# Attention output by channel for pairs of heads, with the probabilities divided before they are turned

## The reference

```python
sc = (q_nope @ k_nope.T + q_rope @ k_rope.T) * scale     # masked by chunks of 64 frames
p = softmax(sc)                                          # p = exp(sc - max) / sum
y_b[:, h] = p @ v[:, h]                                  # queries x 64 channels
y_b = y_b * rsqrt(mean over the 64 channels of y_b ** 2 + eps) * out_norm[G:2 * G]
x = x + concat(y_a, y_b, y_c, y_d) @ w_out
```

## Time and profile before

| | us |
|---|---|
| median of 3 runs | 911.15 (910.9 to 911.25) |
| the profiled execution | 911.08 |
| its span, first to last instruction | 909.3 |
| TensorE busy | 894.7 |
| VectorE, ScalarE, GpSimd busy | 522.9, 220.2, 512.3 |

### The profile page before, as it was taken

One profiled execution on the slowest core, in us unless ns is written; L12 is line 12 of the kernel. 1 busy time (PEld: TensorE's weight loads), 2 busy tenths in 40 slices (PEclk: granted clock), 3 DMA queues, 4 the chain that ended last, 5 costly groups with the idle time before them and its releaser, 6 DMA issues.

```text
span 909.3 us, 15558 instructions
## 1 busy us (share of the span) xinstructions
PE 894.7 (98%) x5980; PEld 815.3 (90%) x5980; DVE 522.9 (58%) x1032; ACT 220.2 (24%) x485; POOL 512.3 (56%) x514
## 2 busy tenths in 40 slices
PE   8999999999999999999999999999999999999998
PEld 6997878678999999999979878866799999999998
DVE  6677858725656565522366776685465656563221
ACT  3334345432000000100133433464300000000001
POOL 6852483315866666666457244902287666666770
PEclk9999999999999999999999999999999999999999
DMA  9969321248554544333444873130855555443421
GB/s 276 275 106 122 90 77 65 52 90 229 139 139 137 140 137 135 128 128 129 129 133 140 31 152 94 48 95 6 185 139 139 140 139 139 140 128 128 142 90 35
DMA packets 159091, 112.92 MB, mean 124 GB/s; under 512 B 9829, under 2 KB 156682, under 8 KB 158890
## 3 DMA queue, kind: packets, MB, share of 16 engines
q1 hardware_dynamic: 154402, 104.44, 40.0%
q0 software_dynamic: 3984, 6.74, 7.2%
q10 hardware_dynamic: 632, 0.75, 0.3%
HBM read 108.33 MB, written 2.27 MB: 122 GB/s over the span
## 4 chain that ended last, share of the span: by engine, by line
PE 86%; DVE 9%; ACT 2%; issue 1%; DMA 1%; SPq 0%; DVEq 0%; ACTq 0%
PE ps L1313 53%; PE ps L899 7%; PE ps L865 6%; PE ps L1272 6%; PE ps L1331 2%; PE ps L885 2%; PE ps L1085 2%; PE ps L1054 1%; PE ps L1117 1%; PE ps L1210 1%; DMA arena<-in_x_sample 1%; PE ps L1218 1%; DVE work L2240 1%; DVE work L2079 1%; DVE arena L2183 0%
## 5 line engine op out<-in xcount | busy, mean ns | idle before, releaser
L674 POOL TENSOR_TENSOR work<-ring 128x512 f32<-128x512 f32 (+1 forms) x66 | 81.8, 1239 | 157.6 <-issue 113.4
L1313 PE MATMUL ps<-mixT,ring 128*128 128x160 f32 x672 | 105.0, 299 | 0.0
L1313 PE MATMUL ps<-hT,work 128*128 128x160 f32 x672 | 98.5, 299 | 0.0
L1313 PE MATMUL ps<-hT,ring 128*128 128x160 f32 x672 | 98.1, 299 | 0.0
L1313 PEld LDWEIGHTS ps<-mixT,ring 128*128 128x128 f32 x672 | 95.8, 190 | 0.0
L1313 PEld LDWEIGHTS ps<-hT,ring 128*128 128x128 f32 x672 | 93.7, 190 | 0.3
L1313 PEld LDWEIGHTS ps<-hT,work 128*128 128x128 f32 x672 | 93.7, 190 | 0.0
L675 POOL TENSOR_TENSOR ring<-ring 128x512 f32<-128x512 f32 (+1 forms) x66 | 82.4, 1248 | 5.2
L677 POOL TENSOR_TENSOR work<-ring,work 128x512 f32<-128x512 f32 (+1 forms) x66 | 82.1, 1244 | 5.2
L676 POOL TENSOR_TENSOR work<-ring 128x512 f32<-128x512 f32 (+1 forms) x66 | 82.0, 1242 | 5.2
L1764 ACT ACTIVATE arena<-ps 128x160 f32<-128x160 f32 x42 | 12.8, 304 | 286.9 <-PE ps L1313 286.9
(11 more groups left out here) (447 smaller groups left out, 1631.5 us busy)
## 6 DMA issues: line engine op xcount, KB each, us to landing
ring<-in_w_gu SPq DMA_DIRECT2D x88, 512.0 KB, 5.2
ring<-in_w_in SPq DMA_DIRECT2D x44, 512.0 KB, 6.4
ring<-in_w_down SPq DMA_DIRECT2D x32, 512.0 KB, 4.5
ring<-in_w_out SPq DMA_DIRECT2D x16, 512.0 KB, 4.9
ring<-in_w_down SPq DMA_DIRECT2D x16, 384.0 KB, 3.8
cst<-in_consts POOLq DMA_DIRECT2D x1, 1664.0 KB, 11.7
ring<-in_w_in SPq DMA_DIRECT2D x2, 640.0 KB, 5.5
arena<-r POOLq DMA_DIRECT2D x8, 160.0 KB, 18.0
```

The lines of the kernel that those rows point to most:

```text
L674: step(tt(s3, a11, a21, ALU.subtract))
L1313: ins = mm(bank(use, at * HT, HT), left, right(k), start=(opens and k == 0 and at == 0), stop=(closes and k == n - 1), skip_group_check=True)
```

## The change

Group B's output is made by channel for two heads at a time, as group C's is. ScalarE gets `shares(h)` behind `exponentials(h)`: it inverts the row sums (Ln, then Exp of the negative) and multiplies the probabilities by them in three parts; the turning waits for that. `weigh_values(p)` runs for heads 0 and 1 in `between(2)` and for heads 2 and 3 after the last head; for that there are two buffers of turned probabilities. ScalarE's `head_squares(p)`, TensorE's `head_mean(p)` and ScalarE's `head_rstd(p)` give 1/rms, and VectorE's `head_result(p)` writes `mixT` tile 2 + p. `b_out`, `group_tail`, `group_tail2`, the turning `bT` and `group_out` for group B go. Product 7 of `rg` moves ahead of the last turning. ScalarE's `exponentials(1)` moves ahead of `conv_input(0)`. On TensorE `pair_mean(1)` and `project(4)` move ahead of the wait for `h_sq`, and on ScalarE `pair_rstd(1)` moves ahead of that square. `pair_out` uses the shared helper `column_pair`; its products stay as they are.

```diff
@@ -155,8 +155,10 @@
...
         u += [(n, (0 if n == "rvt0" else 1,)) for n in fill[h]]
+        if h == 2:
+            u += [("bo0", (7,))]
         if h == H - 1:
-            u += [("rga", (0,)), ("rgb", (1,))]
+            u += [("rga", (0,)), ("rgb", (1,)), ("bm0", (6,))]
...
@@ -164,11 +166,12 @@
...
             u += [("ga0", (6,)), ("gx0_", (2,)), ("ga1", (3,)), ("gx1_", (7,)), ("rgc", (6,))]
-        u += [(f"bo{h}", (7,))]
-    u += [("rkt", (4, 5)), ("bT", (6, 7))]
+        if h == H - 1:
+            u += [("bo1", (7,))]
+    u += [("rkt", (4, 5)), ("bm1", (6,))]
...
     d("lg0", "lg1")
-    u += [("cp0", (4,)), ("cm0", (2,)), ("cp1", (5,)), ("am0", (7,)), ("am1", (6,)), ("cm1", (7,))]
+    u += [("cp0", (4,)), ("cm0", (2,)), ("cp1", (5,)), ("cm1", (7,)), ("am0", (6,)), ("am1", (7,))]
...
@@ -367,6 +370,8 @@
...
         yst = sb("yst", [P, 6, NT * H])
+        pTs = [pT0, work[:, ytm_at + 512:ytm_at + 1536]]
+        bsq = [wt[:, 0, 0:T], pr[:, 640:640 + T]]
...
@@ -991,6 +996,16 @@
...
+            def column_pair(use):
+
+                def both(c, n, left, right, start, stop):
+                    base = banks[use][0] * 512 + c
+                    for a in range(2):
+                        ins = mm(flat[a * HD:(a + 1) * HD, base:base + n], left(a), right(a), start=start, stop=stop,
+                                 skip_group_check=True)
+                    return ins
+                return both
...
@@ -1191,12 +1198,15 @@
...
                         feature("lx1", l, "lx", P, P)
+                        weigh_values(0)
...
                         pair_product("rg", l, 5, opens=True)
+                        pair_product("rg", l, 7, closes=True)
+                        head_mean(0)
...
@@ -1218,17 +1228,24 @@
...
-                def weigh_values(h):
-                    u = f"bo{h}"
+                def weigh_values(p):
+                    u = f"bo{p}"
                     claim(pe, u, l)
-                    need(pe, "pT", l, H, h + 1)
-                    mm(bank(u, 0, 64), pT[:, 0:128], vb[:, 0, h, :], start=True, stop=True)
-                    mm(bank(u, 64, 64), pT[:, 128:256], vb[:, 0, h, :], start=True, stop=False)
-                    mm(bank(u, 64, 64), pT[:, 256:384], vb[:, 1, h, :], start=False, stop=True)
+                    need(pe, "pT", l, H, 2 * p + 2)
+                    both = column_pair(u)
+                    values = lambda i: lambda a: vb[:, i, 2 * p + a, :]
+                    both(0, 256, values(0), lambda a: pTs[a][:, 0:256], True, False)
+                    both(128, 128, values(1), lambda a: pTs[a][:, 256:384], False, False)
+                    both(256, DEC, values(2), lambda a: pTs[a][:, 384:384 + DEC], False, False)
                     for i in range(4):
-                        mm(bank(u, 128, 64, WIDE), pT[:, 512 + i * P:512 + i * P + WIDE], vb[:, 3 + i, h, :],
-                           start=(i == 0), stop=False)
-                    fill(mm(bank(u, 128, 64, WIDE), pT[:, 384:384 + WIDE], vb[:, 2, h, :], start=False, stop=True), u)
+                        ins = both(256, DEC, values(3 + i), lambda a: pTs[a][:, 512 + i * P:512 + i * P + DEC], False, i == 3)
+                    fill(ins, u)
+
+                def head_mean(p):
+                    u = f"bm{p}"
+                    claim(pe, u, l)
+                    need(pe, "b_sq", l, 2, p + 1)
+                    fill(mm(bank(u, 0, T), C("headmean"), bsq[p], start=True, stop=True), u)
...
@@ -1249,13 +1266,12 @@
...
                                 fill(mm(bank(u, 0, AW), w[:, l, t, :], xc[:, t, :], start=True, stop=True), u)
-                        pair_product("rg", l, 7, closes=True)
...
                         turn_out("dT", l, ytm, "y_d")
-                    weigh_values(h)
+                weigh_values(1)
...
@@ -1275,8 +1291,8 @@
                         fill(ins, u)
                 feature("lg0", l, "lg", 0, P)
+                head_mean(1)
                 pair_out(0, l)
-                turn_out("bT", l, ybm, "y_b")
                 pair_scores("c", l, 1)
                 feature("lg1", l, "lg", P, P)
                 pair_mean(0, l)
@@ -1284,12 +1300,12 @@
                 pair_out(1, l)
                 for n in range(1, 4):
                     project(n, (6, 7, 2, 3))
+                pair_mean(1, l)
+                project(4, (6, 7, 2, 3))
                 need(pe, "h_sq", l, 1)
                 for t in range(2):
                     claim(pe, f"am{t}", l)
                     fill(mm(bank(f"am{t}", 0, AW), C("headmean"), an[:, t, :], start=True, stop=True), f"am{t}")
-                project(4, (6, 7, 2, 3))
-                pair_mean(1, l)
                 project(5, (6, 7, 2, 3))
                 for n in range(2):
                     project(n, (0, 1))
@@ -1655,15 +1671,21 @@
...
                                 accum_out=small[:, 140 + 3 * h + n:141 + 3 * h + n])
-                        step(ins, "probs" if n == 2 else None)
+                        step(ins)
                     now_read(act, f"bs{h}")
+                def shares(h):
+                    z, rz = small[:, 140 + 3 * h:143 + 3 * h], small[:, 152 + 3 * h:155 + 3 * h]
+                    step(A(rz, z, ACT.Ln))
+                    step(A(rz, rz, ACT.Exp, scale=-1.0))
+                    for n, (a, w_) in enumerate(((0, 128), (128, 256), (448, 576))):
+                        step(A(pr[:, a:a + w_], pr[:, a:a + w_], ACT.Copy, scale=rz[:, n:n + 1]), "probs" if n == 2 else None)
...
                     wait_filled(act, f"bp{h}", l)
-                    if h > 0:
-                        wait_filled(act, f"bo{h - 1}", l)
+                    if h > 1:
+                        wait_filled(act, "bo0", l)
                     u = f"bp{h}"
-                    step(A(pT[:, :], bank(u, 0, 1024), ACT.Copy), "pT")
+                    step(A(pTs[h % 2], bank(u, 0, 1024), ACT.Copy), "pT")
...
@@ -1691,34 +1713,49 @@
...
+                def head_squares(p):
+
+                    wait_filled(act, f"bo{p}", l)
+                    step(A(bsq[p], bank(f"bo{p}", 0, T), ACT.Square), "b_sq")
+
+                def head_rstd(p):
+
+                    wait_filled(act, f"bm{p}", l)
+                    rsqrt_(l, bsq[p], bank(f"bm{p}", 0, T), 1, name="b_rstd", use=f"bm{p}")
...
                 exponentials(0)
+                shares(0)
...
                 probs_copy(0)
+                exponentials(1)
                 conv_input(0)
-                exponentials(1)
+                shares(1)
...
                 exponentials(2)
+                shares(2)
...
                 conv_input(1)
+                head_squares(0)
...
                 exponentials(3)
+                shares(3)
+                head_rstd(0)
...
                 pair_first("rg")
+                head_squares(1)
...
                 now_read(act, "rkt")
-                need(act, "yms_b", l, 1)
-                rsqrt_(l, yst[:, 4, :], yst[:, 3, :], HD, name="yrstd_b")
...
@@ -1730,6 +1767,7 @@
...
                     step(A(aa[:, t, :], ri[:, 0, t, :], ACT.Exp, scale=c8[:, 2 * l + t:2 * l + t + 1]))
+                head_rstd(1)
...
@@ -1740,12 +1778,12 @@
                 pair_squares(1)
                 need(act, "gelu_arg", l, 1)
                 sigmoid(fl(gg), one_c[:, :], "gelu_sig")
+                pair_rstd(1)
                 need(act, "lru_scanned", l, 1)
                 step(A(fl(an), fl(ah), ACT.Square), "h_sq")
                 for t in range(2):
                     wait_filled(act, f"am{t}", l)
                     rsqrt_(l, aw[:, t, :], bank(f"am{t}", 0, AW), 1, name="a_rstd", use=f"am{t}")
-                pair_rstd(1)
                 squares(l, 1)
                 norm_stat("ms2", l)
@@ -2158,15 +2195,14 @@
...
-                def b_out(h):
-                    need(dve, "probs", l, H, h + 1)
-                    rs3 = small[:, 152 + 3 * h:155 + 3 * h]
-                    step(v.reciprocal(rs3, small[:, 140 + 3 * h:143 + 3 * h]))
-                    wait_filled(dve, f"bo{h}", l)
-                    step(v.tensor_tensor(ybm[:, 0:2, h, :], bank(f"bo{h}", 0, 128).rearrange("p (t e) -> p t e", t=2),
-                                         rs3[:, 0:2].unsqueeze(2).broadcast_to([P, 2, HD]), ALU.mult))
-                    step(v.tensor_scalar(ybm[0:DEC, 2, h, :], bank(f"bo{h}", 128, 64, DEC), rs3[0:DEC, 2:3], None, ALU.mult),
-                         bank_read=(f"bo{h}", l))
+                def head_result(p):
+                    if p == 0:
+                        wait_filled(dve, "rgb", l)
+                    need(dve, "b_rstd", l, 2, p + 1)
+                    step(v.scalar_tensor_tensor(out=mixT[:, 2 + p, :], in0=bank(f"bo{p}", 0, T),
+                                                scalar=col("out_norm", l * KT + 2 + p), in1=bsq[p],
+                                                op0=ALU.mult, op1=ALU.mult), "mix1" if p else None)
+                    now_read(dve, f"bo{p}")
...
@@ -2196,15 +2232,13 @@
```

(34 more changed lines are left out.)

## The result

| | before | after |
|---|---|---|
| median, us | 911.12 (910.9 to 911.25) | 916.25 (915.1 to 916.63) |
| ratio | | 1.0055, interval 1.0037 to 1.0072 |
| span of the profiled execution | 909.3 | 914.5 |
| ScalarE busy, instructions | 220.2, 485 | 241.9, 533 |

What follows compares the result with a forecast made beforehand. TensorE, at work in 98% of the span, paces each layer's first and third stages, VectorE and ScalarE the second. Losses of 0.85 us in layer 0 and 0.45 in layer 1 sum to +1.3 on 911.08: forecast 912.5, range 908.5 to 916.

Steps and rivals of the forecast that it cites:

- part 1: TensorE's work: a pair of heads takes 1.38 us in 28 instructions; TensorE loses 2.0 us of work a layer.
- rival of serial halves: Column halves run one after the other: each pair costs 2.5 us, about +2 a layer, 916 us; chance 0.20.
- no drain is visible: Where TensorE changes to column halves, the trace shows no drain of the engine; the sum would not be altered.
- part 2: ScalarE's shares ahead of each turning: 2.26 us a head; layer 0's turnings 1.9, 2.55, 2.9 and 3.3 us later.
- part 3: Two new waits, before head_result(0) and head_squares(1): in layer 0 gates start 4.55 us late, the big sigmoid 6.75.
- part 4: VectorE's removed group B output work in the second stage: net -4.45 us, so the scans end 2.3 us late.
- part 5: Before the third stage, pair_mean(1) and project(4) move ahead of L1290 and fill its wait; layer 0 ends +0.85 us.
- 20.4 us without gaps: TensorE works unbroken from pair_out(0) at 160.15 us through the moved pieces, so L1290's products start at 180.6.
- gap in stage three: Sign of being wrong: a gap not there before in the layer's last stage, where TensorE's work sets the pace.
- forecast's 0.85: Layer 0's loss in us: products that need group A's rows begin at 184.5 against 183.66.
- Layer 1: Same rows as layer 0, but VectorE is already 0.5 us later there, so the loss is +0.45 us.
- low bound of the shares: Least time of ScalarE's shares for one head: 1.9 us, with L1482's fixed part in place of L1500's.

Runs made afterwards that it cites:

- squares_late: The changed kernel with ScalarE's head_squares(1) moved behind the gates' big sigmoid and the copy of ktm: 913.92 us.
- no_shares_squares_late: The changed kernel without the division by row sums and with head_squares(1) moved behind the big sigmoid and the copy of ktm: 905.09 us.
- old_end: The changed kernel with the old order ahead of the third stage put back (pair_mean(1), project(4), pair_rstd(1), banks): 918.09 us.
- carry_late: The changed kernel with VectorE's carry_c alone moved behind the two gates_in: 916.67 us.
- filler: The changed kernel with eight products of constants added ahead of TensorE's wait for head 0's probabilities: 915.92 us.
- no_first_share: The changed kernel with the division by row sums left out for head 0 alone: 911.48 us.
- before_shares: The kernel before with ScalarE's shares added for each head and copies in place of b_out's reciprocal and two multiplications: 924.47 us.
- squares_carry_late: The changed kernel with head_squares(1) moved behind the copy of ktm and carry_c behind the gates, shares kept: 910.44 us.

## Why the prediction was wrong, point by point

- **TensorE's work (part 1): right in size, with one misreading.** A pair takes 1.39 us (28 instructions from 152.07 us, the next product at 153.46), forecast 1.38. The rival of serial halves is out. But "so no drain is visible" was read from a modelled end of a product. The starts show a delay. The last eight products of `rg` take 1.09 us up to the next start in the kernel before, where full-width products follow, and 1.18 in the change, where column halves follow:

```profile
146.56 1.25 PE L885 MATMUL ps<-work,ring 128*128 128x160 f32 x8
147.65 0.33 PE L1225 MATMUL ps<-arena 128*128 128x64 f32 x2
```

```profile
150.89 1.25 PE L890 MATMUL ps<-work,ring 128*128 128x160 f32 x8
152.07 0.43 PE L1004 MATMUL ps<-arena 128*64 128x256 f32 x1
```

  The Trainium skill (TensorEngine Tiling (Array Packing), Tiling Modes, Key Properties) states that changing the tiling mode drains the engine. The trace agrees that the change costs time, 0.09 us on the way in.
- **The shares (part 2): right in size and in each turning.** 113.42 to 115.64 is 2.22 us, forecast 2.26, and the Trainium skill's figures (ScalarE: Activation LUTs, What ACT_TABLE_LOAD costs) gave an estimated 2.2. The turnings start at 114.74, 126.18, 135.95 and 144.85 us, forecast 114.7, 126.3, 136.1 and 144.8. The wait at head 1 was 1.41 us where two were named.
- **The two new waits (part 3): right in kind, short in size.** VectorE waited 2.00 us for ScalarE (1.5 to 2 named) and ScalarE idled 5.08 (4 to 5). The first gate came 4.96 late, forecast 4.55. The mis-sized term is `carry_c`: 0.24 of hand-over and 1.17 in place of 0.9, since GpSimd worked beside it (the forecast had 0.2 for hand-overs in its 147.6, without naming it). The sigmoid came 7.27 late, forecast 6.75. Of these 0.52 us, 0.25 is the later start of the last `rg` products, and 0.2 that their two took 2.37 us up to the column halves in place of 2.15.
- **What VectorE gives back (part 4):** the last scans end at 180.70, 3.1 us late where 2.3 were forecast. Part 3's 0.5 is carried on, and 4.2 us came back in place of 4.45: `head_result(1)` with its hand-overs takes 0.9 (0.8 forecast), and without `group_out` 1.3 is saved (1.4).
- **The order before the third stage (part 5): right as an edit** (1.8 us over both layers, by two experiments), **wrong in its sum.** The step that failed is "the work from there through the moved pieces takes 20.4 us without gaps". There is a gap of 0.69 us: `pair_mean(0)` waits for its bank, which VectorE reads late. With the 0.53 that `pair_out(0)` started late (160.68 against 160.15) it makes the products of the squares 1.28 us later than forecast (181.88 against 180.6). A gap in stage three was among the prediction's own signs of being wrong, and the rows before could have told it. There the read ends at 163.87 and the product starts at 163.98, with nothing to spare (VectorE's timeline, then TensorE's):

```profile
163.06 0.81 DVE L2240 TENSOR_TENSOR work<-ps,cst 128x384 f32<-128x384 f32 x2
...
163.98 0.81 PE L1028 MATMUL ps<-work,cst 128*128 128x320 f32 x2
```

  By the prediction's own terms VectorE is 6.75 - 2.85 - 1.0 + 0.8 = 3.7 us late at this read. TensorE, 3.9 late at `pair_out(0)` and then free of the turning of `ybm`, is 3.1 late, so an estimated 0.5 of gap follows. Afterwards the read ends at 169.29 by the trace and the product starts at 169.40:

```profile
168.47 0.82 DVE L2272 TENSOR_TENSOR work<-ps,cst 128x384 f32<-128x384 f32 x2
```

  The end of the layer inherits all this: the (0,1) products begin at 185.79, forecast 184.5. Before, they begin at 183.50 and not at 183.66. The sum took the 1.36 us of L1290 as its cost, while the next product starts 1.20 behind it, at 178.66. So they are 2.29 late, where the forecast's 0.85 should have read 1.0.
- **Layer 1:** it was said to lose 0.4 us less than layer 0, and loses 0.57 less (+1.79 against +2.36), for the reason given: its first gate comes 0.54 us less late (41.46 behind the first scores, before 37.04; in layer 0 41.56 and 36.60). The base was 1.3 to 1.5 too low.
- **Small sums:** 153.57 - 150.74 is 2.83 and not 2.85, and the low bound of the shares comes to 2.0 and not 1.9. Neither moves the result.
- **The rest.** Layers 4.15 us against 1.3 forecast. The last us of the median, from 915.1 to 916.25, goes to executions with a late load at the start (916.43 at a clock of 1.000) or with a clock of 0.997 to 0.998. Of neither does the prediction speak.

So the mechanism was the forecast one, and the losses were under-counted: 0.5 up to `pair_out(0)`, about half of it from `carry_c`, and 0.7 for the bank, in each of two layers. The shares, `carry_c` and both orders are shown by experiments. The bank's 0.7 is read from the trace alone; no run takes it out by itself (in squares_late it shrinks to 0.24). Why the clock falls in some executions and not in others stays open. The profiles show that it may fall behind either turning wait, and the kernels without shares, which have no such wait, kept at least 0.999.

## What to carry to other kernels

Here 18 us of work on an engine that is busy for a quarter of the time cost 8 to 9 us, since each piece stood between two steps of the fullest engine. So price work by its place in the hand-over, and ask first whether it is needed at all: a factor ahead of a norm is not, but for the norm's eps. In a queue with a fixed order, put what waits for a late result behind what doesn't, and keep instructions that nobody awaits out of the way of those that release a bank: those two moves with the shares left out gave 901.79 us, 1.0% under the kernel before. When a forecast says "no gaps", go through that stretch bank by bank, with both engines' lag at each: the one that fills the bank and the one that reads it.

## What the runs showed of the hardware

**VectorE beside GpSimd.** One product of `carry_c` (128x128, both inputs in SBUF) takes 293 ns in squares_late, where GpSimd has ended its last rotation 2.7 us earlier, and 901 to 946 ns in no_shares_squares_late, where GpSimd multiplies beside it (`carry_c` by line: duration ns min/median/max, first and last start; first squares_late, then no_shares_squares_late):

```profile
L2180 DVE TENSOR_TENSOR work<-work,cst x4: 293/293/294, 149.8 to 596.1; 128x128 f32<-128x128 f32 x4
```

```profile
L2170 DVE TENSOR_TENSOR work<-work,cst x4: 901/924/946, 142.6 to 585.2; 128x128 f32<-128x128 f32 x4
```

The gates, with one large input and that in PSUM, keep their 0.55 us in the kernel before (143.03 us) and in no_shares_squares_late (144.55 us), each beside a GpSimd product. For `carry_c` it matters which of the two comes first. In the change the first product starts at 147.84 us, just ahead of a GpSimd product at 147.85, and takes 0.29. The second starts at 148.16 and ends at 149.00, 0.15 us behind the end of that GpSimd product, which took 1.00 us where its neighbours take 0.87. The trace thus agrees with a rule of the Trainium skill (SBUF — State Buffer, Who interferes with whom): a VectorE instruction with two SBUF inputs contends with a GpSimd instruction that reads SBUF, and the one that comes second waits for all of the other.

**TensorE's clock.** In six of the profiles (squares_late, old_end, carry_late, filler, no_first_share, before_shares) the granted clock fell to 0.50 (the lower level, 1.2 GHz of 2.4) behind a TensorE wait of 1.4 to 2.9 us before a turning. It came back within 10 us. No fall inside TensorE's work began elsewhere. Most waits of the same length had none behind them: the change's own profile has four, of 1.97, 1.41, 1.94 and 1.41 us, at a clock of 1.00. Where the fall lasted longest, in layer 0 of squares_late and carry_late, the second turning came 3.2 us later (14.66 and 14.64 in place of 11.44 us behind the first). Over the twelve executions of squares_carry_late the time goes with the clock: 909.0 to 909.9 us at 0.999 to 1.000, 910.2 to 911.3 at 0.997 to 0.998, 914.0 and 915.2 at 0.994 and 0.993.
